# Seven products for eight in six of sixteen weight quads of the output projection, and the gain's multiplications on VectorE

## Reference

```python
h    = rmsnorm(x, norm_gain)                       # (256, 4096)
proj = h @ w_in                                    # one combined projection, all branches
mix  = concat(nsa(proj), mlstm(proj))              # (256, 4096), two halves of 2048
y    = x + mix @ w_out                             # w_out (4096, 4096)
out  = rmsnorm(y, final_norm_gain)
```

## Time and profile before

| | |
|---|---|
| median of 3 runs | 1800.57 us (1799.7 to 1801.07) |
| the profiled execution | 1801.2 us, span 1799.2 us |
| busy: PE, VectorE, ScalarE, GpSimd | 1781.6, 1126.8, 844.8, 86.8 us |
| mean granted clock of TensorE | 0.998 |
| read from HBM | 341.38 MB |

### The profile page before, as it was taken

One profiled execution on the slowest core, in us unless ns is written; L12 is line 12 of the kernel. 1 busy time (PEld: TensorE's weight loads), 2 busy tenths in 40 slices (PEclk: granted clock), 3 DMA queues, 4 the chain that ended last, 5 costly groups with the idle time before them and its releaser, 6 DMA issues.

```text
span 1799.2 us, 23389 instructions
## 1 busy us (share of the span) xinstructions
PE 1781.6 (99%) x8196; PEld 1475.6 (82%) x8196; DVE 1126.8 (63%) x1387; ACT 844.8 (47%) x1158; POOL 86.8 (5%) x66
## 2 busy tenths in 40 slices
PE   9999999999999999999999999999999999999997
PEld 7888888888888888888888888888888888888886
DVE  6546545567685766785668566846685875555544
ACT  6645444455554545543444344444444644444443
POOL 0000000001010010100000000000000000000000
PEclk9999999999999999999999999999999999999999
DMA  9657555545455454455555555555555566666654
GB/s 381 236 175 236 178 188 198 181 159 175 150 162 180 149 185 158 164 177 180 193 194 188 180 189 198 187 176 194 192 189 175 186 247 212 207 204 204 206 203 175
DMA packets 97176, 346.88 MB, mean 193 GB/s; under 512 B 10560, under 2 KB 11072, under 8 KB 96704
## 3 DMA queue, kind: packets, MB, share of 16 engines
q1 hardware_dynamic: 94192, 337.22, 55.6%
q10 hardware_dynamic: 2896, 8.39, 1.4%
HBM read 341.38 MB, written 4.19 MB: 192 GB/s over the span
## 4 chain that ended last, share of the span: by engine, by line
PE 93%; DVE 4%; DMA 2%; issue 1%; ACT 1%; DVEq 0%; POOL 0%; SPq 0%; ACTq 0%; POOLq 0%
PE acc_b L502 15%; PE acc_b L504 15%; PE acc_b L503 15%; PE acc_a L502 14%; PE acc_a L503 14%; PE acc_a L504 14%; DMA w_raw<-in_w_all 2%; DVE w_split L1323 1%; DVE ebuf L1376 1%; PE bank_z L765 1%; PE bank_x L503 0%; PE bank_x L504 0%; PE bank_x L502 0%; PE bank_y L618 0%; PE bank_v L503 0%
## 5 line engine op out<-in xcount | busy, mean ns | idle before, releaser
L1323 DVE TENSOR_TENSOR w_split<-w_raw,w_split 128x1024 fp32r<-128x1024 f32 x615 | 770.2, 1256 | 578.3 <-ACT w_split L938 576.0
L938 ACT ACTIVATE w_split<-w_raw 128x1024 fp32r<-128x1024 f32 x615 | 649.4, 1059 | 774.0 <-PE acc_a L504 371.0
L502 PE MATMUL acc_b<-w_split,lhs_hi 128*128 128x512 f32 x1216 | 477.6, 393 | 0.0
L504 PE MATMUL acc_b<-w_split,lhs_lo 128*128 128x512 f32 x1216 | 473.6, 389 | 0.0
L502 PE MATMUL acc_a<-w_split,lhs_hi 128*128 128x512 f32 x1204 | 472.2, 392 | 1.4 <-DVE w_split L1323 1.4
L503 PE MATMUL acc_b<-w_split,lhs_hi 128*128 128x512 f32 x1216 | 473.3, 389 | 0.0
L503 PE MATMUL acc_a<-w_split,lhs_hi 128*128 128x512 f32 x1204 | 469.0, 390 | 0.0
L504 PE MATMUL acc_a<-w_split,lhs_lo 128*128 128x512 f32 x1204 | 469.0, 390 | 0.0
L504 PEld LDWEIGHTS acc_b<-w_split,lhs_lo 128*128 128x128 f32 x1216 | 228.3, 188 | 48.0
L502 PEld LDWEIGHTS acc_b<-w_split,lhs_hi 128*128 128x128 f32 x1216 | 228.4, 188 | 46.5 <-DVE w_split L1323 0.3
L503 PEld LDWEIGHTS acc_b<-w_split,lhs_hi 128*128 128x128 f32 x1216 | 228.5, 188 | 46.0
(11 more groups left out here) (268 smaller groups left out, 861.4 us busy)
## 6 DMA issues: line engine op xcount, KB each, us to landing
w_raw<-in_w_all SPq DMA_DIRECT2D x615, 512.0 KB
wide<-in_x SPq DMA_DIRECT2D x8, 512.0 KB, 10.0
xres<-in_x ACTq DMA_DIRECT2D x8, 512.0 KB, 4.2
out_y<-wide SPq DMA_DIRECT2D x8, 512.0 KB, 3.1
gained_x<-in_x_cols_first SPq DMA_DIRECT2D x2, 1024.0 KB, 10.7
toe<-in_toe_bias ACTq DMA_DIRECT2D x4, 512.0 KB, 6.1
gain_f<-in_final_norm_gain ACTq DMA_DIRECT2D x1, 2048.0 KB, 12.3
gained_x<-in_x_cols_first SPq DMA_DIRECT2D x2, 512.0 KB, 8.3
```

The source lines that it names most:

```text
L502: pe.matmul(dst, a[0], b[0], start=start, stop=False)
L504: return pe.matmul(dst, a[1], b[0], start=False, stop=stop)
L938: act.activation(w_hi[:, cols], w_raw[:, cols], ACT.Copy).then_inc(hi_done, 1)
L1323: dve.tensor_tensor(w_lo[:, cols], w_raw[:, cols], w_hi[:, cols].bitcast(F32), ALU.subtract).then_inc(lo_done, 1)
```

## The change

Output blocks 1 to 6 run as three twos (`TWOS`; blocks 2p+1 and 2p+2). Their pairs alternate in the stream. For one k pair, the four weight tiles of the two blocks, with the 2 x 2 tiles of the activations (token tile t, k tile k), form a 2 x 2 matrix product. For k pairs 0 to 5 (`SEVEN`) it is formed by seven products (Winograd's form of Strassen's algorithm), for the other ten by eight as before. The order of the k pairs is 6, 7, 0, 8, 1, 9, 2, 10, 3, 11, 4, 12, 5, 13, 14, 15. A two uses all eight banks: four hold the outputs' own sums (`own`), four the sums of the products P1, P5, P6 and P7 that several outputs share (`seven`). The sets are exchanged from one two to the next.

Sums of activations (S1 to S4) are made and split once, on VectorE and ScalarE, in the second block of the last mLSTM head. Sums of weights (T1 to T4) are made for each quad on VectorE from `w_raw`, and split as the weights are. Of the second pair of a quad only one tile is split as it is. After a two, VectorE combines the shared sums (`shared_sums`, over steps 30, 31 and 0, 1 of the next) and adds the own ones (`own_sums`, steps 2 and 3). The output loops, before partly rolled, are written out.

The load of `gain_f` moves to step 29 of the last two, the residuals' loads to step 6 (two at once, after the first block's squares). The gain's multiplications move from GpSimd to VectorE, eight pieces (`gain_piece`) in steps 8 to 15 of the last block.

```diff
+TWOS = 3
+SEVEN = tuple(range(6))
+ORDER = (6, 7, 0, 8, 1, 9, 2, 10, 3, 11, 4, 12, 5, 13, 14, 15)
 ...
 # PE
+            def seven(p, j):
...
+                pe.wait_ge(a_lo_done, n + 1)
+                passes(shared[P1][:, :], x_tile(0, 0), w_tile(0, 0), first, final)
+                passes(own[0][0][:, :], x_tile(0, 1), w_tile(0, 1), False, False).then_inc(pe_used, 1)
+                pe.wait_ge(t13_lo, n + 1)
+                passes(shared[P5][:, :], x_sum(S1), w_sum(0), first, final)
+                passes(shared[P7][:, :], x_sum(S3), w_sum(1), first, final)
+                pe.wait_ge(lo_done, q + 2)
+                passes(own[1][0][:, :], x_sum(S4), w_tile(1, 1), False, False).then_inc(pe_used, 1)
+                pe.wait_ge(t24_lo, n + 1)
+                passes(own[0][1][:, :], x_tile(1, 1), w_sum(2), False, False)
+                passes(shared[P6][:, :], x_sum(S2), w_sum(3), first, final).then_inc(t_used, 1)
...
 # ScalarE
+            def split_seven(p, j):
...
+                act.wait_ge(pe_used, q - RING + 1)
+                act.wait_ge(w_loaded[s], LOADED * (q // RING + 1))
+                act.activation(w_hi[:, cols], w_raw[:, cols], ACT.Copy).then_inc(hi_done, 1)
+                act.wait_ge(t13_raw, n + 1)
+                act.wait_ge(t_used, n) if n else None
+                act.activation(t_hi[:, 0:2 * BW], t_raw[:, 0:2 * BW], ACT.Copy).then_inc(t13_hi, 1)
+                act.wait_ge(pe_used, q - RING + 2)
+                act.activation(w_hi[:, cols], w_raw[:, cols], ACT.Copy).then_inc(hi_done, 1)
+                act.wait_ge(lo_done, q + 1)
+                act.activation(t_hi[:, 2 * BW:]..., t_raw..., ACT.Copy).then_inc(t24_hi, 1)
+            def two_pieces(r):
+                if r == 6 and p == 0:
+                    squares(0); residuals(0)
+                elif r == 6:
+                    act.wait_ge(eight_free, p)
+                    squares(2 * p - 1)
+                    residuals(p)                  # behind seven_free; in the last block one load
+                elif r == 8 and p:
+                    squares(2 * p)
+                elif r == 29 and p < TWOS:
+                    act.wait_ge(t_used, (p + 1) * len(SEVEN))
+                    act.activation(x1_copy[:, :], banks(p)[1][P1][:, :], ACT.Copy)
+                    if p == TWOS - 1:
+                        act.dma_start(gain_f[:, :], ...)
...
 # VectorE
+            def lo_seven(p, j):
+                for h in range(2):
+                    dve.wait_ge(w_loaded[s + h], LOADED * (q // RING + 1))
+                if n:
+                    dve.wait_ge(t24_lo, n)
+                T1, T3 raw (1024)             .then_inc(t13_raw, 1)
+                dve.wait_ge(t13_raw, n + 1);   T2 raw (512)    .then_inc(t2_raw, 1)
+                dve.wait_ge(hi_done, q + 1);   weights_lo(0, 0, 2).then_inc(a_lo_done, 1)
+                dve.wait_ge(t13_hi, n + 1);    T1, T3 lo (1024).then_inc(t13_lo, 1)
+                dve.wait_ge(t13_lo, n + 1);    T4 raw (512)    .then_inc(lo_done, 1)
+                dve.wait_ge(hi_done, q + 2);   weights_lo(1, 1, 1).then_inc(lo_done, 1)
+                dve.wait_ge(t24_hi, n + 1);    T2, T4 lo (1024).then_inc(t24_lo, 1)
...
 # GpSimd
-            with pool.Fori(0, N_OUT - 1) as n:
-                pool.wait_ge(sq_done, n + 1)
-                for t in range(TT):
-                    dst = res[:, t, bass.ds(n * BW, BW)]
-                    last = pool.tensor_tensor(dst, dst, gain_f[:, bass.ds(n * BW, BW)], ALU.mult)
```

More of the change, by code:

```diff
@@ L300, in small_parts, with banks @@
                 "p (k j n) -> p k j n", j=2, n=N_SMALL)
+        def banks(p):
+            a, b = [acc[0][0], acc[0][1], bx, bv], [acc[1][0], acc[1][1], by, bz]
+            own, seven = (b, a) if p % 2 == 0 else (a, b)
+            return (own[0:2], own[2:4]), seven
         def halves(t):
@@ L898, in _, with eight @@
-            out_pairs(N_OUT - 2, 0, range(PAIRS))
-            out_pairs(N_OUT - 1, 1, range(PAIRS - RING))
+            def eight(p, j, h):
+                q = TWO0 + p * TWO_STEPS + 2 * j + h
+                s, c = q % RING, ORDER[j]
+                pe.wait_ge(lo_done, q + 1)
+                for t in range(TT):
+                    for k in range(2):
+                        kk = 2 * c + k
+                        cols = slice((2 * s + k) * BW, (2 * s + k + 1) * BW)
+                        toks = slice(t * P, (t + 1) * P)
+                        last = passes(banks(p)[0][h][t][:, :],
+                                      (lhs_hi[:, kk, toks], lhs_lo[:, kk, toks]),
+                                      (w_hi[:, cols], w_lo[:, cols]), j == 0 and k == 0,
+                                      j == PAIRS - 1 and k == 1)
+                last.then_inc(pe_used, 1)
@@ new lines, in _ @@
+            pe.wait_ge(s_lo_done, 1)
+            for p in range(TWOS):
+                if p == 0:
+                    pe.wait_ge(acc0_free, B_OUT)
+                    pe.wait_ge(acc1_free, B_OUT)
+                else:
+                    pe.wait_ge(seven_free, p)
+                for j in range(PAIRS):
+                    if ORDER[j] not in SEVEN:
+                        eight(p, j, 0)
+                        eight(p, j, 1)
+                        continue
+                    if ORDER[j] == SEVEN[0]:
+                        if p == 0:
+                            pe.wait_ge(out0_free, 1)
+                            pe.wait_ge(out1_free, 1)
+                        else:
+                            pe.wait_ge(eight_free, p)
+                    seven(p, j)
@@ L901, in _ @@
+            pe.wait_ge(seven_free, TWOS)
+            for c in range(PAIRS - RING):
+                pair(N_OUT - 1 + B_OUT, c, 0)
             for t in range(TT):
@@ L905, in _ @@
                     for k in range(2):
-                        last = wide(1, t, 2 * c + k, c % RING, k)
+                        last = wide(0, t, 2 * c + k, c % RING, k)
                     if t == 1:
@@ L1223, in silu_gate, with head @@
                                ).then_inc(mz_e, 1)
-            def head(h, blocks, last={}):
+            def head(h, blocks, last={}, before={}):
                 b, pieces = 4 * h + B_MLSTM, head_pieces(h)
                 pieces[3] = {1: [lambda: silu_gate(h)]}
-                for c, late in last.items():
-                    pieces[2].setdefault(c, []).extend(late)
+                for n, more in ((1, before), (2, last)):
+                    for c, late in more.items():
+                        pieces[n].setdefault(c, []).extend(late)
                 stage_free = ((tr_done, h + (T_MQK + 1)), (v_split_lo, h + 3), None,
@@ L1266, in _ @@
                     act.wait_ge(ym_done, HEADS_M)
+                    act.wait_ge(s_lo_done, 1)
                     fetch_residual(0, 0)
[L1268 to L1279, removed]
@@ L1288, in _ @@
+            for r in range(LOOKAHEAD, TWOS * TWO_STEPS + PAIRS):
+                p, j, h, few = two_step(r) if r < TWOS * TWO_STEPS else (None, None, 0, False)
+                two_pieces(r)
+                if not few:
+                    q = TWO0 + r
+                    split(q, q % RING, LOADED * (q // RING + 1))
+                elif h == 0:
+                    split_seven(p, j)
+            act.wait_ge(sq_done, N_OUT - 1)
+            act.wait_ge(out0_free, 2)
             square(0, N_OUT - 1).then_inc(sq_last, 1)
-            act.wait_ge(gained, N_OUT - 1)
+            act.wait_ge(gained, 1)
@@ new lines, in input_sum_lo @@
+            def input_sum_lo(f):
+                dve.wait_ge(s_hi_done, SUM_ORDER.index(f) + 1)
+                last = dve.tensor_tensor(s_lo[:, f], s_raw[:, f], s_hi[:, f].bitcast(F32), ALU.subtract)
+                if f == SUM_ORDER[-1]:
+                    last.then_inc(s_lo_done, 1)
+            sums = {SUMS - 2 + i: [lambda f=f: input_sum(f)] for i, f in enumerate(SUM_ORDER)}
+            for i, f in enumerate(SUM_ORDER):
+                sums.setdefault(SUMS + 1 + i, []).append(lambda f=f: input_sum_lo(f))
@@ L1771, in add_residual @@
+            head(HEADS_M - 1, 3, {c + 2: [lambda c=c: mix_lo(c)] for c in range(MIX_EARLY)}, sums)
+            def add_residual(n, full, turn, tiles=range(TT)):
+                cols = slice(n * BW, (n + 1) * BW)
                 for t in tiles:
                     if t == 0:
-                        dve.wait_ge(acc0_full, n + (B_OUT + 1))
-                        dve.wait_ge(xr_in[i], turn)
+                        dve.wait_ge(acc0_full, full)
+                        dve.wait_ge(xr_in[0], turn)
@@ L1800, in final_sum @@
+            for r in range(LOOKAHEAD, TWOS * TWO_STEPS + PAIRS):
+                p, j, h, few = two_step(r) if r < TWOS * TWO_STEPS else (None, None, 0, False)
+                two_pieces(r)
+                if not few:
+                    q = TWO0 + r
+                    lo(q, q % RING)
+                elif h == 0:
+                    lo_seven(p, j)
             def final_sum(t):
```

244 lines of the change are left out of this document (197 added, 47 removed).

## The result

The changed kernel takes 1788.07 us (median of 4 runs, 1787.77 to 1788.90) against 1800.82 us (4 runs, 1799.70 to 1802.22). The ratio is 0.9929, 95% interval 0.9917 to 0.9941: 0.7% faster. The forecast was 1788.3 us, range 1787.0 to 1796.0. One of the four executions of the kernel of experiment 6 took 3628.33 us, twice the others, for no reason that any run shows; the time given there is the median of the other three.

The account below looks back on a forecast made before the run. TensorE was taken as the bound, busy 1781.6 of 1799.2 us. The 1801.2 us execution less 12.24 of matmuls gives 1789.0, on the median's footing 1788.3 us, all else priced at nothing; range 1787.0 to 1796.0.

Parts of the forecast that it names:

- The gain is the matmuls: On PE in the three twos: 21 matmuls for 24 in six of sixteen quads, 12.24 us off, the whole gain.
- Prices on VectorE: VectorE's instruction times in a two: 6.6 us a seven, 72.4 of 82.96 us in all, so it fits at 87%.
- "gain is eaten" rival: Strided sums on VectorE cost 2.30 us, a turn needs 11.5: 1801.2 us, no change; chance 0.08.
- The steady turn: A seven then an eight-quad, the tightest stretch: paced by PE at 10.20 us, with 3.2 us of cover for T2/T4's low parts.
- my 2.2: Entry of a two, step 6: 2.2 us of cover, the least found, behind ScalarE's squares and issue of residual loads.
- Landing: Weight-ring loads in a turn: the second of two lands 3.5 us after its issue; ends 2.8 and 6.7 us.
- paced by the loads: Weight ring in a turn: loads set the pace once 5.6 us plus landing exceeds 10.2, from a landing of 4.6 us.
- The 2 MB load of the gain: Moved to step 29 of the last two: priced at nothing, up to 3.5 us if cover were gone.
- GpSimd's removal: GpSimd's fourteen gain multiplications removed: they cost PE nothing, but slow VectorE.
- my figure of 2.3 us for a disturbed split: A VectorE split that overlaps GpSimd's pair of gain multiplications takes 2.30 us for 1.23.
- Idles from bank changes and the clock: PE's bank changes in sevens: 0.5 us at most, taken as nothing; rival of a lowered clock, about 1913 us, chance 0.02.
- The section of the Trainium skill named in the prediction: "A second HAM failure mode: psum-queue depth-cycling": turning through PSUM banks each round can leave small idles that swing PE's clock.

Follow-up runs that it names:

- experiment 6: Changed kernel with a two's six sevens consecutive and the first tile pair's low parts made for 256 of 1024 columns: 1825.54 us, ratio 1.0137 to before.
- the eighth product's 299.69 us: Changed kernel with product P2 issued twice in each of the 18 sevens, so 24 matmuls a quad again: 1800.74 us, ratio 0.9999 to before.
- the line through zero, three and six: Changed kernel with zero (P2 issued twice), three or six sevens in a two: 1800.74, 1794.56 and 1788.07 us.
- experiment 7: Changed kernel with useless 1.26 us VectorE repeats per seven, before (early) or behind (late) the slots' last reads: one late 1789.98, early 1800.32; two late 1810.24, early 1825.07 us.
- experiment 3: Kernel before with only the gain's multiplications moved from GpSimd to VectorE, in steps 8 to 15 of the last block: 1801.04 us, ratio 1.0001.
- experiment 4: Changed kernel with the gain's eight multiplications on GpSimd in the last block: 1790.26 us, ratio 0.9943 to the kernel before.
- experiment 5: Changed kernel with the six sevens of a two one after the other: 1827.73 us, ratio 1.0150 to the kernel before.

## Why the prediction was right

- **The gain is the matmuls**, 12.24 us. Shown three ways: 12.25 between the residual sums, the eighth product's 299.69 us, and the line through zero, three and six.
- **Prices on VectorE**: 72.4 us a two was forecast, 69 to 71 is busy. Spaced operands cost nothing, so the "gain is eaten" rival falls. Its size was plausible: one extra 1.26 us a seven at the wrong place takes the whole gain (experiment 7).
- **The steady turn** is 10.20 us on PE and its cover 3.2 us, both as predicted. At the entry to the second two, split 6 ended at 1578.65 and PE took it at 1581.69: 3.0 us of cover for my 2.2, because the issue of the residual loads runs beside the squares and not behind them.
- **Landing was mis-sized, the weak term.** I took 3.5 us for the second of two loads. In the fifteen turns T1/T3 raw waited nine times, 5.1 us in all (seven, 4.4 us, are filed under the load and two under "issue"), and went on 4.1 to 5.0 us after the second issue. Three times that was above 4.6, the mark that I gave for "paced by the loads": 4.83, 4.98 and 4.86. But a late T1/T3 raw hardly reaches PE. Of the 1.3 us by which five turns of the first two exceed 51.0, 0.9 is in the first, at the squares, with no wait for a load; the other twelve turns of the three twos take 10.24 us on average, PE's 10.20. The cover of the T2/T4 low parts is lowest where the longest wait was, and it is 2.7 us there for 3.2:

```profile
1534.28 1.23 DVE L2014 TENSOR_TENSOR t_lo<-t_raw,t_hi 128x1024 fp32r<-128x1024 f32 x1 [0.53 <-ACT t_hi L1409]
...
1538.17 0.39 PE L562 MATMUL acc_b<-t_hi,lhs_hi 128*128 128x512 f32 x1
```

  The mechanism was right and the landing too short. The forecast did not hang on the 3.5: with 5.0 us in each turn, the prediction's own sum makes 5 x 0.4 = 2.0 us a two, inside even the 2.2 of cover that I had at the entry. That is little room.
- **The 2 MB load of the gain**, priced at nothing or at most 3.5 us of cover, made ScalarE wait 4.64 us at one split. PE did not wait.
- **GpSimd's removal**: no gain by itself (experiment 3), as forecast. In experiment 4 my figure of 2.3 us for a disturbed split was too small: it took up to 3.42.
- **Idles from bank changes and the clock**: PE turns through seven banks in each seven at 0.227 us a matmul, without an idle, at a granted clock of 1.00. The section of the Trainium skill named in the prediction speaks of small idles between groups of matmuls; in the changed kernel there are none. Where experiments made PE wait between banks, twice a seven and up to 1.57 us in experiment 5, the clock stayed at 1.00 too. It fell once, behind the wait of 2.30 us in experiment 7.
- **The 0.9 us of the spans** outside the changed part were not foreseen. They lie in the first 58 us, where each engine waits for its first loads. VectorE begins to take the first block's results at 57.4 to 58.3 us in the ten traces with the changed kernel's program and at 58.75 and 58.80 in the two with the old one's. By the first residual sum the groups overlap: 1482.41 to 1483.71 us for 1483.55 and 1483.69. How much of it is the program and how much the spread from run to run stays open.

## What to carry to other kernels

When one engine bounds a kernel and the others have room, fewer products at the price of more sums can pay their matmuls in full, as here, if the sums are spread: the same work bunched cost 40 us, three times the gain. Count not only an engine's time but the path on which it holds a buffer of a ring, and what another engine's queue has ahead of the next piece: 1.26 us there cost 12 us in all, and 2 us behind it. Test the margin with a useless repeat at either place, it tells which of the two is near its limit.

## What the runs showed of the hardware that was not expected

- Two loads of 512 KB issued 0.6 us apart: in the nine turns in which VectorE waited for them, it went on 4.1 to 5.0 us after the second's issue, three times at 4.8 us or more. In three others they were there within 3.9 to 4.0 us. Traffic in one of the long cases ran from 1503 to past 1506, at 250, 389, 352 and 127 GB/s, so the last microsecond moved little. Why the landings differ is open.
- VectorE's subtraction of 1024 float32 columns takes up to 3.42 us for 1.23 beside a GpSimd that multiplies without a pause, and GpSimd's eight pieces take 23.6 us, where the same 14 x 512 columns took it 17.8 us in the kernel before.
- A stop costs PE about 0.3 us more than the wait that the profile lists (experiment 5: 0.79 for 0.51).
- After one wait of 2.30 us PE ran at a granted clock of 0.50 for some 3 us; after waits of 1.76 us in the same run it stayed at 1.00.
